# A two-layer decoder step: the RMS norm of the second layer's tokens is moved from the second input projection into the first output projection

## The reference, cut to what matters

```
x1 = x0 + mix0 @ w_out0                      # end of layer 0  (combine)
h  = x1 * rsqrt(mean(x1*x1) + 1e-6) * norm_w[1]
z1 = h @ w_in1                               # 1024 -> 4096    (project_hgrn)
... HGRN2 recurrence over z1 -> mix1 ...
y  = rms_norm(x1 + mix1 @ w_out1, final_norm_w)
```

## Time and profile before

| | us |
|---|---|
| median of 3 runs (lowest, highest) | 3370.96 (3368.59, 3375.1) |
| the profiled execution, its own time | 3382.41 |
| span of the profiled execution | 3380.6 |
| PE busy | 3118.2 (92%) |
| DVE busy | 1480.3 (44%) |
| ACT busy | 1046.0 (31%) |
| POOL busy | 1108.9 (33%) |

### The profile page before, as it was taken

The page is one execution under the profiler, slowest core; times in us unless marked ns, Lnnn a source line. Parts: engine busy times, 40 slices in busy tenths (PEclk is TensorE's granted clock), DMA queues, the critical chain, the costliest instruction groups (busy, mean ns, idle before and its releaser), DMA issues. The chain is left out here.

```text
span 3380.6 us, 45840 instructions
## 1 busy us (share of the span) xinstructions
PE 3118.2 (92%) x16972; PEld 2728.9 (81%) x16972; DVE 1480.3 (44%) x2861; ACT 1046.0 (31%) x1749; POOL 1108.9 (33%) x678
## 2 busy tenths in 40 slices
PE   6999999799999698789699978999979999997999
PEld 6999899688888588576588858999978888886786
DVE  6999344204420477654300004124344544446542
ACT  4111122312211345431200002025445444455651
POOL 1323222132223455450212211245425343345442
PEclk9999999899999799888899998999979998998899
DMA  4434655455542455533522213233334333333333
GB/s 129 105 121 129 193 172 159 109 123 167 170 132 87 171 184 180 187 135 109 203 76 98 99 60 101 88 120 121 110 108 144 99 123 125 107 122 116 129 121 110
DMA packets 373868, 434.44 MB, mean 129 GB/s; under 512 B 46000, under 2 KB 314928, under 8 KB 364512
## 3 DMA queue, kind: packets, MB, share of 16 engines
q1 hardware_dynamic: 277648, 373.05, 34.8%
q10 hardware_dynamic: 96080, 59.49, 5.8%
HBM read 285.26 MB, written 151.39 MB: 129 GB/s over the span
## 5 line engine op out<-in xcount | busy, mean ns | idle before, releaser
L780 PE MATMUL p_psum<-p_h_hi,p_w_hi 128*128 128x344 f32 (+1 forms) x1600 | 568.2, 355 | 0.0
L780 PE MATMUL p_psum<-p_h_hi,p_w_lo 128*128 128x344 f32 (+1 forms) x1600 | 562.3, 351 | 0.0
L780 PE MATMUL p_psum<-p_h_lo,p_w_hi 128*128 128x344 f32 (+1 forms) x1600 | 560.8, 350 | 0.0
L2435 PE MATMUL p_psum<-p_h_hi,p_w_hi 128*128 128x344 f32 (+1 forms) x1280 | 464.9, 363 | 0.0
L2435 PE MATMUL p_psum<-p_h_lo,p_w_hi 128*128 128x344 f32 (+1 forms) x1280 | 458.1, 358 | 0.0
L2435 PE MATMUL p_psum<-p_h_hi,p_w_lo 128*128 128x344 f32 (+1 forms) x1280 | 457.7, 358 | 0.0
L364 POOL CAST p_w_hi<-p_w_raw 128x1024 fp32r<-128x1024 f32 x80 | 88.8, 1110 | 821.2 <-PE p_psum L780 675.6
L780 PEld LDWEIGHTS p_psum<-p_h_hi,p_w_hi 128*128 128x128 f32 x1600 | 302.8, 189 | 36.5 <-issue 9.3
L780 PEld LDWEIGHTS p_psum<-p_h_hi,p_w_lo 128*128 128x128 f32 x1600 | 302.8, 189 | 29.1
L780 PEld LDWEIGHTS p_psum<-p_h_lo,p_w_hi 128*128 128x128 f32 x1600 | 302.9, 189 | 28.5
L2195 DVE COPY p_out<-p_psum 128x344 f32<-128x344 f32 (+1 forms) x160 | 93.7, 586 | 488.9 <-PE p_psum L2435 488.8
(11 more groups left out here) (333 smaller groups left out, 6060.7 us busy)
## 6 DMA issues: line engine op xcount, KB each, us to landing
p_w_raw<-in_w_in SPq DMA_DIRECT2D x144, 512.0 KB, 4.8
z<-p_out ACTq DMA_DIRECT2D x64, 512.0 KB, 3.6
z<-p_out SPq DMA_DIRECT2D x64, 512.0 KB, 3.2
p_raw<-z SPq DMA_DIRECT2D x32, 1024.0 KB, 5.5
rg_raw<-z SPq DMA_DIRECT2D x16, 1536.0 KB, 8.2
c_m_raw<-m SPq DMA_DIRECT2D x16, 1024.0 KB, 6.9
p_xt<-x SPq DMA_DIRECT2D x32, 512.0 KB, 4.0
u_s<-p_out SPq DMA_DIRECT2D x128, 73.0 KB, 3.1
```

Of the source, the lines that this page charges most:

```text
L780: ins = pe.matmul(bank, wv[par][:, k, :], h[:, k, c0:c0 + n], start=(k == 0 and j == 0), stop=(k == KD - 1 and j == 2))
L2435: ins = pe.matmul(bank, wv[par][:, k, :], h[:, k, c0:c0 + n], start=(k == 0 and j == 0), stop=(k == KD - 1 and j == 2))
```

## The change

In `combine`, each tile's sum is now followed by its norm: ACT stores `xo`, squares it into `xn`, takes the root; DVE takes the reciprocal and multiplies into `xn`; ACT stores `xn` to a new scratch tensor `x1n`. `wrow` and the two `xn` buffers lie in the three staging slots of the weights, so that `wrow` is loaded after the weights are split. In `project_hgrn`, the preludes load `x1n` instead of `x1`, and neither square nor multiply. Four slots (`xt[0]`, `xt[1]`, `xn[0]`, `xn[1]`) take the loads, each reloaded when its tile is turned. The loads of the first four tiles of half B stand at step 0. Prelude B uses two pairs of banks (0,1 and 2,3) and the first strip of half B waits for its last low part. The row of norm weights is no longer among the block's constants.

```diff
-def combine(nc, tag, mix, n_k, w_out, x_in, x_out, final_w=None):
+def combine(nc, tag, mix, n_k, w_out, x_in, x_out, norm_w):
...
+        wrow, xn = staging[0], staging[1:3]
...
             sp.wait_ge(w_lo_done, n_k)
+            sp.dma_start(wrow[:], norm_w.unsqueeze(0).broadcast_to([P, D])).then_inc(const_ld, 16)
             for par in range(2):
                 sp.dma_start(xi[par][:], x_in["x"][par, :, :]).then_inc(x_ld[par], 16)
...
+                dve.wait_ge(rms_done, t + 1)
+                dve.reciprocal(stat[par][0:n, 2:3], stat[par][0:n, 1:2]).then_inc(rstd_done, 1)
+                dve.wait_ge(rstd_done, t + 1)
+                dve.scalar_tensor_tensor(out=xn[par][0:n, :], in0=xo[par][0:n, :],
+                                         scalar=stat[par][0:n, 2:3], in1=wrow[0:n, :],
+                                         op0=ALU.mult, op1=ALU.mult).then_inc(y_done, 1)
             tiles(dve, tile)
...
                 dst = x_out["x"][t, :, :] if n == P else x_out["s"]
                 act.dma_start(dst, xo[par][0:n, :]).then_inc(stored[par], 16)
+                act.wait_ge(xn_st[par], i * 16 + CREDIT)
+                act.activation(xn[par][0:n, :], xo[par][0:n, :], ACT.Square, scale=D ** -0.5,
+                               accum_out=stat[par][0:n, 0:1]).then_inc(sq_done, 1)
+                act.wait_ge(sq_done, t + 1)
+                act.activation(stat[par][0:n, 1:2], stat[par][0:n, 0:1], ACT.Sqrt, bias=eps[0:n, :])\
+                    .then_inc(rms_done, 1)
+                act.wait_ge(y_done, t + 1)
+                dst = x_out["xn"][t, :, :] if n == P else x_out["xns"]
+                act.dma_start(dst, xn[par][0:n, :]).then_inc(xn_st[par], 16)
...
-    N_CONST = 6
+    N_CONST = 5
...
         def tp_view(hf, par, n):
-            b = 4 + 2 * par if hf == 0 else 2
+            b = 4 + 2 * par if hf == 0 else 2 * par
...
                 no = no_of(hf, t)
-                if no >= 2:
-                    sp.wait_ge(xn_done, no - 1)
-                sp.dma_start(xt[no % 2][0:n, :], x_in["x"][tile, :, :] if n == P else x_in["s"])\
-                    .then_inc(x_ld[no % 2], 16)
+                if no >= 4:
+                    sp.wait_ge(tp_done, no - 3)
+                sp.dma_start(x_slot[no % 4][0:n, :], x_in["xn"][tile, :, :] if n == P else x_in["xns"])\
+                    .then_inc(x_ld[no % 4], 16)
...
             for k in range(OUT + N_OUT):
+                if k == 0:
+                    for t in tiles_of(1)[:4]:
+                        load_x(1, *t)
                 if k == BEFORE_B:
-                    for t in tiles_of(1):
+                    for t in tiles_of(1)[4:]:
                         load_x(1, *t)
...
             def prelude(hf):
-                tiles = tiles_of(hf)
-                square_x(hf, *tiles[0])
-                for front, back in zip(tiles[1:], tiles):
-                    square_x(hf, *front)
-                    high(hf, *back)
-                high(hf, *tiles[-1])
+                for t in tiles_of(hf):
+                    high(hf, *t)
...
-                    pe.wait_ge(xn_done, no + 1)
-                    if hf == 0 and no >= 2:
+                    pe.wait_ge(x_ld[no % 4], 16 * (no // 4 + 1))
+                    if t >= 2:
                         pe.wait_ge(lo_done, no - 1)
-                    if hf and t:
-                        pe.wait_ge(lo_done, no)
...
-                    if s == 0:
+                    if s == 0 and hf:
+                        pe.wait_ge(lo_done, N_A + NTH)
+                    elif s == 0:
```

More of the change, by code:

```diff
@@ L862, in combine @@
         xo = [sb(f"xo{i}", [P, D]) for i in range(2)]
[L863 to L867, removed]
+        stat = [sb(f"stat{i}", [P, 3]) for i in range(2)]
+        eps = sb("eps", [P, 1])
         psum = ctx.enter_context(nc.psum_tensor(f"{tag}_psum", [P, 2, 2, BLK], F32))
@@ L872, in combine @@
         slots = [x[:] for x in staging + xi + xo]
+        wrow, xn = staging[0], staging[1:3]
         w_ld, m_ld = [sem(f"w_ld{i}") for i in range(len(slots))], [sem(f"m_ld{i}") for i in range(2)]
-        x_ld, stored = [sem(f"x_ld{i}") for i in range(2)], [sem(f"stored{i}") for i in range(2)]
+        x_ld, stored, xn_st = ([sem(f"{n}{i}") for i in range(2)] for n in ("x_ld", "stored", "xn_st"))
         w_hi_done, w_lo_done, m_hi_done, m_lo_done = (sem(n) for n in ("w_hi_done", "w_lo_done", "m_hi_done", "m_lo_done"))
@@ L888, in _ @@
         def _(sp):
-            if final_w is not None:
-                sp.dma_start(wrow[:], final_w.unsqueeze(0).broadcast_to([P, D])).then_inc(const_ld, 16)
             for k in range(n_k):
@@ L948, in _ @@
         def _(dve):
-            if final_w is not None:
-                dve.memset(eps[:], RMS_EPS).then_inc(eps_set, 1)
+            dve.memset(eps[:], RMS_EPS).then_inc(eps_set, 1)
             for k in range(n_k):
@@ L955, in _ @@
             dve.sem_inc(sum_done, 2)
-            if final_w is not None:
-                dve.wait_ge(const_ld, 16)
+            dve.wait_ge(const_ld, 16)
             def tile(t, i, par, n):
@@ L977, in _ @@
                 act.sem_inc(stored[par], CREDIT)
+                act.sem_inc(xn_st[par], CREDIT)
             for k in range(n_k):
@@ L983, in _ @@
                     act.activation(m_hi[k][:], m_raw[k][:], ACT.Copy).then_inc(m_hi_done, 1)
-            if final_w is not None:
-                act.wait_ge(eps_set, 1)
+            act.wait_ge(eps_set, 1)
+            act.wait_ge(w_lo_done, n_k)
             def high(t, i, par, n=P):
@@ L1015, in _ @@
             finish(NT, NT // 2, 0, NS)
-            act.wait_ge(stored[0], 16 * (NT // 2 + 1) + CREDIT)
-            act.wait_ge(stored[1], 16 * (NT // 2) + CREDIT)
+            for done in (stored, xn_st):
+                act.wait_ge(done[0], 16 * (NT // 2 + 1) + CREDIT)
+                act.wait_ge(done[1], 16 * (NT // 2) + CREDIT)
 def retention_glu(nc, a, z, y_dram, mix, out_p, out_s):
@@ L1689, in project_hgrn @@
         ps_turn, ps_score, ps_o, ps_s = (ps[:, b, :].rearrange("p (s c) -> p s c", c=P) for b in range(4, 8))
+        x_slot = [xt[0], xt[1], xn[0], xn[1]]
         s_state = [v[:].rearrange("p (n c) -> p n c", c=P) for v in (xt[0], xt[1], xn[0], xn[1])]
@@ L1708, in project_hgrn @@
         const_ld = sem("const_ld")
-        x_ld, w_ld, stored = ([sem(f"{n}{i}") for i in range(2)] for n in ("x_ld", "w_ld", "stored"))
+        x_ld = [sem(f"x_ld{e}") for e in range(4)]
+        w_ld, stored = ([sem(f"{n}{i}") for i in range(2)] for n in ("w_ld", "stored"))
         ld, mix_st = ([sem(f"{n}{i}") for i in range(2)] for n in ("ld", "mix_st"))
@@ L1714, in project_hgrn @@
         m_ld, xi_ld, y_st = ([sem(f"{n}{i}") for i in range(2)] for n in ("m_ld", "xi_ld", "y_st"))
-        names = ("sq_done", "rms_done", "rstd_done", "eps_set", "xn_done", "tp_done", "hi_done", "lo_done", "w_hi_done",
+        names = ("eps_set", "tp_done", "hi_done", "lo_done", "w_hi_done",
                  "w_lo_done", "blk_done", "ev_done")
-        (sq_done, rms_done, rstd_done, eps_set, xn_done, tp_done, hi_done, lo_done, w_hi_done, w_lo_done, blk_done,
+        (eps_set, tp_done, hi_done, lo_done, w_hi_done, w_lo_done, blk_done,
          ev_done) = (sem(n) for n in names)
@@ L1801, in _ @@
                 sp.dma_start(w_raw[par][:], a["w_in1"][par]).then_inc(w_ld[par], 16)
-            sp.dma_start(wrow[:], a["norm_w"][1].unsqueeze(0).broadcast_to([P, D])).then_inc(const_ld, 16)
             for d, s in ((ident, "ident"), (causal, "causal"), (eye8, "eye8"), (bounds, "hg_bounds"),
@@ L2032, in _ @@
         def _(act):
[L2033 to L2042, removed]
             def high(hf, t, tile, n):
@@ L2159, in _ @@
         def _(dve):
[L2160 to L2167, removed]
             def lower(hf, t, tile, n):
@@ L2176, in prelude @@
             def prelude(hf):
[L2177 to L2182, removed]
+                for t in tiles_of(hf):
+                    lower(hf, *t)
             def evict(g, blocks):
@@ L2589, in program @@
     m1 = {"z": scratch("m1", [NT, P, KD, P]), "zs": scratch("m1s", [P, KD, NS])}
-    x1 = {"x": scratch("x1", [NT, P, D]), "s": scratch("x1s", [NS, D])}
+    x1 = {"x": scratch("x1", [NT, P, D]), "s": scratch("x1s", [NS, D]),
+          "xn": scratch("x1n", [NT, P, D]), "xns": scratch("x1ns", [NS, D])}
     y5 = scratch("y5", [2, KD * P, L8, YCH])
@@ L2595, in program @@
     retention_glu(nc, a, z0, y5, m0, o["ret_p"], o["ret_s"])
-    combine(nc, "c0", m0, 16, a["w_out0"], x0, x1)
+    combine(nc, "c0", m0, 16, a["w_out0"], x0, x1, a["norm_w"][1])
     project_hgrn(nc, a, x1, z1, m1, o["hg_p"], o["hg_s"], {"x": o["y_p"], "s": o["y_s"]})
```

2 lines of the change are left out of this document (1 added, 1 removed).

## The result

| | before | after |
|---|---|---|
| median | 3373.03 (3368.59 to 3378.75) | 3347.51 (3345.05 to 3348.59) |
| ratio, 95% interval | | 0.9912 [0.9892, 0.9931] |
| profiled span | 3380.6 | 3343.2 |

A forecast was written before the change was run, and what follows sets the result against it. PE was taken to set the pace in combine, with two holes in the preludes where PE does little. Terms +3.4 - 16.1 - 13.7 = -26.4 us, from 3370.96 to 3344.6 us, range 3335 to 3356.

The forecast's parts named there:

- Combine, 16 tiles at 0: In combine, all tiles but the last: the added norm hides behind PE and costs 0.
- The last tile, +3.4: At the end of combine: nothing hides the last tile's norm and second store, costing 3.4 us, bounds 3.0 to 4.7.
- Prelude A, -16.1: Projection's first prelude: earlier start and two tiles per 4.41 us round gain 16.1 us, bounds 12 to 18.
- Prelude B, -13.7: Half B's prelude: two tiles share a round, cutting 31.94 us to 18.2, gain 13.7, bounds 11 to 16.8.
- The granted clock rises inside the preludes: Rival, both preludes: busier PE gets the upper clock, rounds fall to 3.5, -6 us more, 3338; chance 0.15.
- the round of 4.41 us: In both preludes: transposes, high part and low part take 4.41 us at the lower clock, for two tiles.
- Loads bound the preludes: Rival, both preludes: tiles wait for loads, 3.0 us per tile, A 6.4 more and B 2 more, 3353; chance 0.17.
- one of my signs of being wrong: In the preludes: the forecast is wrong if loads stand in front of the transposes after tile 3.
- Slower through combine: Rival, combine: the norm's chain exceeds the 21.8 us of a tile; at 24.5 us the time is 3388; chance 0.04.
- given back in the steps: Rival, steps behind prelude B: the gain is lost there, whole to within 0.2%; chance 0.04.
- The early loads at step 0: SP's queue: four half-B loads moved to step 0 pass in idle time, 1.6 us of issue, cost 0.

The follow-up runs named there:

- the norm added alone: The kernel before, with combine of the changed kernel, its norm read by nobody and the projection norming again; ratio to before 1.0006 [0.9995, 1.0018].
- One pair each: The changed kernel with a single pair of banks in each prelude; ratio to the kernel before 1.0006 [0.9995, 1.0016].
- two slots: The changed kernel with two load slots instead of four and two early loads instead of four; ratio to the kernel before 0.9942 [0.9924, 0.9961].
- two pairs alone: The kernel before, with prelude B in two pairs of banks, norm still in the prelude; ratio to before 0.9989 [0.9977, 1.0].
- norm twice: The changed kernel with the square and multiply of each combine tile done twice; ratio to the kernel before 0.9897 [0.9871, 0.9922].
- strip waits less: The changed kernel with prelude B's bank pairs exchanged and a shorter wait for the first strip; ratio to the kernel before 0.9884 [0.9868, 0.9901].
- no early loads: The changed kernel with all eight loads of half B at step 7, none at step 0; ratio to the kernel before 0.9904 [0.9885, 0.9924].

## Why the prediction was right, and where its sizes were off

**Combine, 16 tiles at 0: right.** Shown by the norm added alone (1.0006) and by the doubled norm. My 9 us of work per tile was on the safe side: the multiply ends 7.7 us after PE's end of the tile.

**The last tile, +3.4: right.** Measured 6.28 - 2.79 = 3.49. There is no table load, as the copies, squares and roots of prelude A had suggested.

**Prelude A, -16.1: the right mechanism, the term too small.** It was 43.1 - 23.6 = 19.5. Tile 0's transposes began 7.1 us after the first issue, where counting bytes up to `head_w` had given 8.4: 1.3 us. The rest of the stretch was 16.5 us where I had 4 x 4.41 + 1.0 = 18.6: two rounds of 3.5 instead of 4.4, and 0.4 less for the 8 rows at the upper clock. The bounds of this term, 12 to 18, did not hold it. The upper one had the clock but no room for an earlier start.

**Prelude B, -13.7: the same.** It was 31.9 - 15.6 = 16.4. Every round ran at the upper clock; it is the end of my range (16.8) less the 0.4 that the last load was late. The new wait of the first strip cost 1.5, and the granted clock had sometimes fallen by then.

**The rivals.** "The granted clock rises inside the preludes" is what happened; I had given it 0.15 and 6 us. The stretches add up to 3.49 - 19.5 - 16.4 = -32.4, and that is 6 us beyond my sum, but the agreement of the two sixes is luck: 1.3 of it is the earlier start of A, and in A only two of four rounds ran at the upper level, where that rival had all four. The term that was mis-sized is the round of 4.41 us. The lower clock of the earlier trace rows was carried over into preludes in which PE is used twice as closely, and the rounds at the upper level took 3.5. One pair each, where the clock held down in A and fell at the third tile of B, says that the spacing matters. "Loads bound the preludes" would have come true with two slots. In the changed kernel loads cost up to 0.8 us at the last tile of B, one of my signs of being wrong, in small, and up to 0.95 us at tile 1 of A. "Slower through combine" has nothing in the runs. Nor has "given back in the steps": from the first strip of half B to the end it is 878.0 us before and 874.8, 869.0 and 873.7 after. The early loads at step 0, which I costed at 0, are also worth 0. The range was added up loosely: -18 and -32 from 3370.96 with 5 more on each side is 3334 to 3358, not 3335 to 3356.

**What the parts are worth.** In prelude B (31.9 us before) the second pair alone gives 4.7 us, the norm's move alone 1.2, both with two slots 9.1, all of it 15.9 to 16.6. Each part lifts a limit that the others leave in place, so the parts don't add up. In the ratio, two pairs alone are 4 us, which a test of that edit by itself would have dismissed; both with two slots are 20, and all of it 30 to 36. That does not hold for the move as a whole, since prelude A had its second pair already.

Still open: where the scatter between executions comes from. The three ratios (30, 36 and 35 us) do not contradict the 32.4 of the stretches, which lies in all three intervals. Parts that the kernels share differ between profiles as well: in the three of the changed kernel the sample sum is stored at 2009.0, 2013.0 and 2008.3 us, and the time from the first strip of half B to the end differs by 5.8 us. Up to 2.7 of that is the 48 matmuls behind prelude B, and there are more such places behind them; no run here separates them.

## What to carry to other kernels

When a stage is one chain through several engines, list for each item all that the next one waits for (engine, bank, buffer, load), and price the change with each of them as the limit: in prelude B the producer's move alone gave 1.2 us and the second pair of banks alone 4.7, but both with four load slots 16. And when an experiment takes a part out, check that it doesn't take out something that the kernel before already had. Work moved into a stage where PE is full and the others idle is free but for the last item, which has nobody to hide behind. When the edit packs PE's work closer, don't take the granted clock from the old profile: price both levels. A single profile can't tell an edit's effect from the clock's where the clock rises at another place each time.

## What the runs showed of the hardware that was not expected

**DVE's multiply waits for POOL's subtraction, inside its own row.** In combine of the changed kernel:

```profile
1770.35 4.61 POOL L913 TENSOR_TENSOR c_m_lo<-c_m_raw,c_m_hi 128x2048 fp32r<-128x2048 f32 x1 [17.15 <-ACT c_m_hi L986]
...
1771.87 4.17 DVE L964 SCALAR_TENSOR_TENSOR c_staging<-c_xo,c_stat,c_staging 128x1024 f32<-128x1024 f32 x1
```

The multiply takes 4.17 us and ends at 1776.04, 1.08 after POOL's end at 1774.96. Its median over the 17 tiles is 3.87 us. The same multiply with POOL idle takes 1.28 for a full tile and 1.27 for the sample tile. The kernel before shows it once, in the first tile of prelude A: 2.34 us, and again an end 1.08 us after that of a POOL subtraction.

```profile
2028.20 2.35 POOL L1953 TENSOR_TENSOR p_w_lo<-p_w_raw,p_w_hi 128x1024 fp32r<-128x1024 f32 x1
2029.29 2.34 DVE L2165 SCALAR_TENSOR_TENSOR p_xn<-p_xt,p_stat,p_wrow 128x1024 f32<-128x1024 f32 x1
```

In the window of combine the 14 multiplies have 50.6 us, where 14 x 1.28 is 17.9. So of DVE's 70 us there some 33, nearly half, is waiting that the profile counts as busy. With the multiply doubled, DVE's busy time rose only from 70 to 74.5 us: the first of the two began 1.2 us later, behind the doubled square, and so waited less. The Trainium skill (SBUF — State Buffer, "SBUF: two separate sides") describes this as a lock held for a whole instruction when DVE reads two tensors from SBUF against a POOL instruction that reads SBUF; the rows agree. It cost nothing here, as the tile has 21.8 us.

**The same kernel finds the clock up at different tiles.** Prelude A reached the upper level at tile 4, 3 and 3 in three profiles of the changed kernel. In three kernels that differ nowhere in that stage it was tile 2 (norm twice), 3 (strip waits less) and 7 (no early loads).
